# One decoder step on one core: common tile offsets, a turned output, uneven filling and another order of loads

## The reference, cut to what matters

```python
pp = in_proj(rmsnorm(x, norm_g), w_in, ...)            # 1024 -> 14 groups of columns
def block(i):                                          # forgetting attention: 8 heads x 64, blocks of 128 queries
    sc = einsum('bqhd,bkhd->bhqk', qb, k) * scale + cq[..., None] - c[:, :, None, :]
    sc = where(kpos[None, :] <= qpos[:, None], sc, -inf)
    p = softmax(sc, axis=-1)
    return einsum('bhqk,bkhd->bqhd', p, v)
o_hg, s = hgrn2(...)                                   # gated linear recurrence, 4 heads, state 128x128
o_mem = mem_attn(mem_q, mk, mv)                        # attention into 256 memory tokens
ya = (o_fox * silu(fox_z)) @ w_pa                      # and yb, ym likewise
mixed = sigmoid(ga) * ya + sigmoid(gb) * yb + sigmoid(gm) * ym
y = rmsnorm(x + mixed @ w_o, final_norm_g)
```

## Time and profile before

| | |
|---|---|
| median of three executions | 2919.84 us (2919.51 to 2931.8) |
| profiled execution | 2921.01 us, span 2919.3 |
| busy: TensorE | 2777.6 us, 95% |
| busy: VectorE, ScalarE, GpSimd | 1555.2, 1026.5, 766.0 us |
| mean granted TensorE clock | 0.986 |
| read from and written to HBM | 411 and 112 MB |

### The profile page before, as it was taken

How to read it: one execution, slowest core, us unless ns; L and a number is a source line. 1 busy time by engine, 2 the same in 40 slices (tenths; PEclk the granted TensorE clock), 3 DMA queues, 4 the chain that set the end, 5 groups by cost and what they waited for, 6 DMA issues and landing times.

```text
span 2919.3 us, 38536 instructions
## 1 busy us (share of the span) xinstructions
PE 2777.6 (95%) x13880; PEld 2279.4 (78%) x13880; DVE 1555.2 (53%) x2995; ACT 1026.5 (35%) x1946; POOL 766.0 (26%) x731
## 2 busy tenths in 40 slices
PE   7899998999999999899799999999999999999998
PEld 5778877777777878687688877888888877888887
DVE  6413566543442576765456555556554654544444
ACT  1211110333332444453355445455454332323231
POOL 6038775134225352523020041010020134000000
PEclk9999999999999999999999999999999999999999
DMA  5667678656646666655754565455344564333331
GB/s 174 227 234 228 224 241 282 247 170 187 190 156 218 207 203 222 213 186 192 239 177 131 158 200 166 145 173 164 120 155 173 195 228 165 112 123 109 126 104 41
DMA packets 285612, 525.78 MB, mean 180 GB/s; under 512 B 110238, under 2 KB 119007, under 8 KB 263151
## 3 DMA queue, kind: packets, MB, share of 16 engines
q1 hardware_dynamic: 226383, 309.16, 34.2%
q10 hardware_dynamic: 54720, 201.19, 19.8%
q0 software_dynamic: 4320, 12.98, 1.3%
HBM read 410.82 MB, written 112.41 MB: 179 GB/s over the span
## 4 chain that ended last, share of the span: by engine, by line
PE 70%; DMA 7%; POOL 6%; DVE 4%; issue 3%; SPq 3%; ACT 2%; ACTq 0%; POOLq 0%; DVEq 0%
PE fill_out L2623 21%; PE fox_o_sum L345 4%; PE fox_turned L391 4%; PE in_out L98 4%; PE in_out L100 4%; PE in_out L99 4%; PE mf_out L100 3%; PE mf_out L98 3%; PE mf_out L99 3%; POOL dc_slot L1660 2%; PE fox_scores L379 2%; DMA fill_x<-x_tiles 2%; PE mf_fin L98 2%; PE mf_fin L100 2%; PE mf_fin L99 2%
## 5 line engine op out<-in xcount | busy, mean ns | idle before, releaser
L2623 PE MATMUL fill_out<-keep_hi,fill_x 128*128 128x512 f32 x2112 | 734.8, 410 | 31.0 <-DMA fill_x<-x_tiles 15.8
L2623 PEld LDWEIGHTS fill_out<-keep_hi,fill_x 128*128 128x128 f32 x2112 | 386.2, 190 | 104.2 <-issue 20.8
L2623 PE MATMUL fill_out<-keep_lo,fill_x 128*128 128x512 f32 x1056 | 432.8, 410 | 0.0
L498 DVE TENSOR_TENSOR fox_pt_lo<-fox_turned,fox_pt_hi 128x512 fp32r<-128x512 f32 (+1 forms) x320 | 194.8, 609 | 183.5 <-ACT fox_pt_hi L443 181.6
L443 ACT ACTIVATE fox_pt_hi<-fox_turned 128x512 fp32r<-128x512 f32 (+1 forms) x320 | 169.9, 531 | 303.1 <-PE fox_turned L391 301.5
L2250 ACT ACTIVATE in_stage<-in_out 128x512 f32<-128x512 f32 (+1 forms) x119 | 70.9, 597 | 553.3 <-PE in_out L100 508.9
L2723 POOL CAST keep_hi<-fill_raw 128x512 fp32r<-128x512 f32 x72 | 48.8, 678 | 733.7 <-PE fill_out L2633 705.1
L484 DVE CUSTOM_DVE_ANT_0 fox_probs<-fox_scores,fox_bias 128x512 f32<-128x512 f32 (+2 forms) x320 | 187.5, 608 | 98.3 <-PE fox_scores L380 55.9
L2623 PEld LDWEIGHTS fill_out<-keep_lo,fill_x 128*128 128x128 f32 x1056 | 201.0, 190 | 31.8
L391 PE MATMUL fox_turned<-ident,fox_probs 128*128 128x128 f32 x1088 | 172.7, 274 | 14.9 <-ACT fox_probs L434 14.9
L391 PEld LDWEIGHTS fox_turned<-ident,fox_probs 128*128 128x128 f32 x1088 | 128.6, 140 | 44.9 <-ACT fox_probs L434 20.0
(11 more groups left out here) (395 smaller groups left out, 6396.8 us busy)
## 6 DMA issues: line engine op xcount, KB each, us to landing
fill_x<-x_tiles ACTq DMA_DIRECT2D x130, 1024.0 KB, 5.5
dc_slot<-in_cache_fox_k_dram SPq DMA_DIRECT2D x128, 256.0 KB, 3.7
dc_slot<-in_cache_fox_v_dram SPq DMA_DIRECT2D x128, 256.0 KB, 3.4
in_raw<-in_w_in_dram SPq DMA_DIRECT2D x104, 256.0 KB, 4.1
plain<-fill_stage ACTq DMA_DIRECT2D x96, 256.0 KB, 5.1
turned<-in_stage ACTq DMA_DIRECT2D x64, 256.0 KB, 3.8
fill_raw<-in_w_in_dram SPq DMA_DIRECT2D x56, 256.0 KB, 2.9
mf_g_in<-gated SPq DMA_DIRECT2D x51, 256.0 KB, 3.0
```

Source lines behind the costliest of these rows:

```text
L498: dve.tensor_tensor(pt_lo[:, b, skip:BANK], bank_of(st)[:, skip:BANK], pt_hi[:, b, skip:BANK].bitcast(F32), ALU.subtract).then_inc(turned_ ...
L2623: ins = pe.matmul(self.out[n % self.OUTS][:], x, w, start=(k == 0 and term == 0), stop=(ends and term == 2))
```

## The change

Four edits, independent of each other.

- **Offsets.** `bound` and `rest` become parts of one tile of 128 bytes; `xs_both` is followed by a tile of 448 bytes; `stat` moves behind the tiles that it shifted; in the attention `halves` goes and `pt_hi`, `pt_lo` and `o_turned` stand directly behind `probs`; `pages_begin` has 1024 bytes instead of 512. `keep_*`, `x_first`, `rest_*`, `fill_x`, all matmul operands of the attention and of the merge's products then start 256 bytes past a multiple of 512. `dc_pr` stays at 32 and 64 modulo 128.
- **Turning back.** L406's four matmuls become four transposes against the identity. VectorE copies the first halves of the four blocks to `o_rows`, adds the second halves, frees the bank, and then does its four products in place, from SBUF.
- **Filling.** `deal` gives the 1552 matmuls out by shares: 7 for the last slot of each quad, 2 for every other.
- **SyncE.** The loads of `w_o`'s slices move from GpSimd's queue to SyncE's: slices 0 and 1 once GpSimd has split the early weights, slices 2v+2 and 2v+3 at unit v, each waiting for the split of the slice two before. `load_g(3)` comes right behind `load_g(2)`. `load_w` 8 and 9 come at unit 1, 10 and 11 at unit 2.

```diff
-        self.bound, self.rest = (ctx.enter_context(nc.sbuf_tensor(n, [P, HH], F32)) for n in ("bound", "rest"))
+        limits = ctx.enter_context(nc.sbuf_tensor("limits", [P, LINE], F32))
+        self.bound, self.rest = limits[:, 0:HH], limits[:, HH:2 * HH]
...
-        fill.begin(first_matmuls + fill.spread(matmuls, 2 * FH * J_HEAD) + last_matmuls)
+        shares = [SEAM if st == ("key", st[1], st[2], 4 * st[2] + 3) and half else 2
+                  for st in steps if st[0] == "key" for half in range(2)]
+        fill.begin(first_matmuls + fill.deal(matmuls, shares) + last_matmuls)
...
+    def deal(matmuls, shares):
+        edges = [matmuls * sum(shares[:n]) // sum(shares) for n in range(len(shares) + 1)]
+        return [b - a for a, b in zip(edges, edges[1:])]
...
-                        last = pe.matmul(bank_of(st)[:, t * P:(t + 1) * P], o_turned[:, t * P:(t + 1) * P], halves[:],
-                                         start=True, stop=True)
+                        last = pe.transpose(bank_of(st)[:, t * P:(t + 1) * P], o_turned[:, t * P:(t + 1) * P],
+                                            core.ident[:])
...
+                    halves = bank_of(st)[:].rearrange("p (t u d) -> p t u d", u=2, d=FD)
+                    dve.tensor_copy(o_rows[n % 2][:], halves[:, :, 0, :]).then_inc(halves_added, 1)
+                    dve.wait_ge(halves_added, 2 * n + 1)
+                    dve.tensor_tensor(o_rows[n % 2][:], o_rows[n % 2][:], halves[:, :, 1, :], ALU.add
+                                      ).then_inc(halves_added, 1)
+                    dve.wait_ge(halves_added, 2 * n + 2)
+                    dve.sem_inc(turned_used, 1)
...
-                                                        in0=bank_of(st)[:, t * P:t * P + FD],
+                        last = dve.scalar_tensor_tensor(out=o_rows[n % 2][:, t, :], in0=o_rows[n % 2][:, t, :],
...
-                    dve.wait_ge(rows_ready, n + 1)
-                    dve.sem_inc(turned_used, 1)
...
+            def load_last(i):
+                kk, n = last_slices[i]
+                k = kk - NB * BT
+                if i >= 2:
+                    sp.wait_ge(late_split, 2 * i - 2)
+                sp.dma_start(late_raw[i % 2], w_o[k * P:(k + 1) * P, n * BANK:(n + 1) * BANK]
+                             ).then_inc(late_loaded[i % 2], 16)
...
+            sp.wait_ge(early_split, 2 * EARLY)
+            for i in range(2):
+                load_last(i)
...
             load_g(2)
+            load_g(3)
...
-                    if t == 0 and u == 0:
-                        for i in range(2 * BT, len(slices) - EARLY):
-                            load_w(i)
+                    if 1 <= v <= 2:
+                        for i in range(BT // 2):
+                            load_w((2 * BT + (v - 1) * BT // 2) + i)
...
-                    if u % HALVES == 1 and s + 3 < SEQ:
+                    if u % HALVES == 1 and 4 <= s + 3 < SEQ:
                         load_g(s + 3)
+                    for i in range(2 * v + 2, min(2 * v + 4, len(last_slices))):
+                        load_last(i)
...
-                if i + 2 < len(last_slices):
-                    pool.wait_ge(late_split, 2 * i + 2)
-                    load(i + 2)
...
+            held.enter_context(nc.sbuf_tensor("xs_end", [P, -KT * SAMPLE_COLUMNS % P], F32))
```

More of the change, by code:

```diff
@@ L31 @@
 BANK = 512
+LINE = 32
 NEG = -1e30
@@ L111, in attend_prompt @@
     S_BANKS, TURN_BANKS, PT_SLOTS = 2, 3, 4
-    SPREAD = 0.8
+    SPREAD, SEAM = 0.8, 7
     DEPTH = 2
@@ L175, in attend_prompt @@
         mask_r, ident_r = sb("mask_r", [P, P], F32R), sb("ident_r", [P, P], F32R)
-        halves = sb("halves", [P, P])
         probs = sb("probs", [P, PROBS])
+        pt_hi, pt_lo = sb("pt_hi", [P, PT_SLOTS, BANK], F32R), sb("pt_lo", [P, PT_SLOTS, BANK], F32R)
+        o_turned = sb("o_turned", [P, BANK])
         most = sb("most", [P, 8, CHUNKS[-1]])
@@ L181, in attend_prompt @@
         inverse = sb("inverse", [P, 4])
-        pt_hi, pt_lo = sb("pt_hi", [P, PT_SLOTS, BANK], F32R), sb("pt_lo", [P, PT_SLOTS, BANK], F32R)
-        o_turned = sb("o_turned", [P, BANK])
         def psum(name, n):
@@ L212, in attend_prompt @@
         o_copied, rows_ready = sem("o_copied"), sem("rows_ready")
-        started, inverse_ready = sem("started"), sem("inverse_ready")
+        started, inverse_ready, halves_added = sem("started"), sem("inverse_ready"), sem("halves_added")
         def slots_of(st):
@@ L316, in _ @@
             link(pool.memset(mask[:], 0.0))
-            link(pool.memset(halves[:], 0.0))
             pool.affine_select(out=mask[:], in_=mask[:], compare_op=ALU.is_ge, fill=NEG, base=0,
-                               pattern=[[-1, P]], channel_multiplier=1)
-            for n, base in enumerate((0, -FD, FD)):
-                link(pool.affine_select(out=halves[:], in_=halves[:], compare_op=ALU.not_equal, fill=1.0,
-                                        base=base, pattern=[[-1, P]], channel_multiplier=1))
+                               pattern=[[-1, P]], channel_multiplier=1).then_inc(masked, 1)
+            pool.wait_ge(masked, 1)
             link(pool.tensor_copy(mask_r[:], mask[:]))
@@ L509, in _ @@
                     dve.wait_ge(turned_ready, turn_at[st] + 1)
+                    halves = bank_of(st)[:].rearrange("p (t u d) -> p t u d", u=2, d=FD)
[5 more added lines that the diff above has]
+                    dve.sem_inc(turned_used, 1)
                     for t in range(4):
-                        last = dve.scalar_tensor_tensor(out=o_rows[n % 2][:, t, :],
-                                                        in0=bank_of(st)[:, t * P:t * P + FD],
+                        last = dve.scalar_tensor_tensor(out=o_rows[n % 2][:, t, :], in0=o_rows[n % 2][:, t, :],
                                                         scalar=inverse[:, t:t + 1], in1=z[n % 2][:, t, :],
@@ L2302, in normalise_and_project @@
         normed = [sb(f"normed{r}", [P, D]) for r in range(2)]
-        gains, memory_gains, stat = sb("gains", [P, D]), sb("memory_gains", [P, D]), sb("stat", [P, 2, 3])
+        gains, memory_gains = sb("gains", [P, D]), sb("memory_gains", [P, D])
         raw = [sb(f"raw{r}", [P, W]) for r in range(RAWS)]
@@ L2306, in normalise_and_project @@
         stage = [sb(f"stage{s}", [P, W]) for s in range(STAGES)]
+        stat = sb("stat", [P, 2, 3])
         turned = [ctx.enter_context(nc.psum_tensor(f"np_turned{r}", [P, KT, P], F32)) for r in range(TR)]
@@ L2575, in spread @@
         return [matmuls * (n + 1) // slots - matmuls * n // slots for n in range(slots)]
+    @staticmethod
+    def deal(matmuls, shares):
+        edges = [matmuls * sum(shares[:n]) // sum(shares) for n in range(len(shares) + 1)]
+        return [b - a for a, b in zip(edges, edges[1:])]
     def left(self):
@@ L2883, in merge_and_finish @@
         late_hi, late_lo = (sb(f"late_{n}", [P, len(slices) - EARLY, BANK], F32R) for n in ("hi", "lo"))
-        sb("pages_begin", [P, P])
+        sb("pages_begin", [P, 2 * P])
         early_hi, early_lo = (sb(f"early_{n}", [P, EARLY, BANK], F32R) for n in ("hi", "lo"))
@@ L2996, in _ @@
         def _(pool):
-            def load(i):
-                kk, n = last_slices[i]
-                k = kk - NB * BT
-                pool.dma_start(late_raw[i % 2], w_o[k * P:(k + 1) * P, n * BANK:(n + 1) * BANK]
-                               ).then_inc(late_loaded[i % 2], 16)
             def load_early(i):
@@ L3021, in _ @@
             pool.wait_ge(early_split, 2 * EARLY)
-            for i in range(2):
-                load(i)
             memory.multiplied(pool)
```

2 lines of the change are left out of this document (1 added, 1 removed).

## The result

The changed kernel takes 2907.69 us (median of 14 runs) against 2923.23 us of the kernel before on the same chip: a ratio of 0.9948, 95% interval 0.9936 to 0.996, or 15.2 us less (12 to 19). The forecast was 2882, with a range from 2864 to 2902. So it is faster, by under half of what was forecast, and the time lies outside the range. The kernel before took 2919.84 us when the prediction was made and 2923.23 in these runs, so some 3 us of the distance to 2882 are not the change's.

A forecast was written before the change was run, and what follows sets the result against it. The prediction took TensorE to bound the kernel; -17.8 - 14.0 + 2.5 - 9.0 + 0 = -38.3 took the profiled 2921.0 us to 2882.7, and with the median 1.2 lower to 2882 us, range 2864 to 2902.

The forecast's parts named there:

- What bounds the kernel: Whole kernel: TensorE holds 70% of the chain that ended last, no other engine more than 7%.
- Term 1: Common tile offsets for matmul operands throughout the kernel shorten the spacing between matmuls: -17.8 us.
- The 1702 inside: x 3.5 ns = 6.0 us: Attention: each of its 1702 fill matmuls gains 3.5 ns from common offsets, 6.0 us in all.
- the values product's 0.8: Attention: 640 matmuls of probabilities with values gain 1.2 ns each from common offsets, 0.8 us.
- its discount: Offsets' saving of 20.9 us of TensorE time: 15% left to stretches where it waits for something else.
- rival A: Offsets don't matter anywhere, so their gain is absent: 2899 us; chance 0.17.
- Term 2: Attention's back steps: transposes replace four products, -14.0 us on TensorE; the sum of halves moves to VectorE, +2.5 us.
- +2.5 on VectorE: Attention's back steps: VectorE's added copy and addition delay what is queued behind them, between 0 and 15 us, taken as +2.5.
- rival B: Attention: ScalarE and VectorE take the gain back, VectorE costing 12 us instead of 2.5: 2902 us; chance 0.13.
- In the short ones: Attention's short quads: scores come 2 to 3 a step, so some of VectorE's extra time shows.
- Term 3: Attention's quad seams: uneven filling covers TensorE's waits for the last exponential, -9.0 us, between -3 and -12.
- Term 4: Merge's begin: SyncE's new load order turns holes of 8.4 and 2.7 us into three smaller ones, 0 us.

The follow-up runs named there:

- the three kernels above: Tiles moved only, against the kernel before: starts 320 and 192 (2918.53 us against 2921.49), 0 and 256 (2906.42 against 2916.56), or the change's 256 and 256.
- kernel with late products: Kernel before plus offsets, transposes and filling, SyncE's order as before, VectorE's four products one key step later: 2886.97 us, ratio 0.9900.

## Why the prediction was wrong

The time lies 26 us above 2882. Some 3 of these are the slower kernel before; the gain itself was 15.2 us instead of 38.3. By the steps:

- **What bounds the kernel**: right, as far as shown. The offsets and the filling, which gave TensorE less to do or to wait for, gained; for the transposes alone the interval reaches just past 0.
- **Term 1, offsets, -17.8: the failed part is "The 1702 inside: x 3.5 ns = 6.0 us"** and the values product's 0.8. Outside the sum held by the rows: 4.4 ns for a kept fill matmul (233.4 to 229.0 in the recurrence) instead of 5.8, 6 in the projection and the first pass, about 12 us together, as forecast after its discount. In the attention, where 5.8 us were forecast after the discount, the profiles show 1.5 us for all its matmuls, within that stage's noise. That accounts for 4.3 of the 9.0 us by which the term missed: the timing has only 8.8, up to 12.6, of these 13.5 us, and what became of the rest stays open. The prediction took 227 ns as the spacing of tiles with one offset and 230 as that of the attention. Rows show something else, a merge run of tiles with one offset behind four transposes:

```profile
2501.51 0.60 PE L3057 MATMUL mf_turned<-ident,mf_g_in 128*128 128x128 f32 x4
2501.86 0.48 PE L100 MATMUL mf_out<-mf_early_hi,mf_t_hi 128*128 128x512 f32 x1
2502.17 0.40 PE L101 MATMUL mf_out<-mf_early_hi,mf_t_lo 128*128 128x512 f32 x1
...
2504.03 0.39 PE L100 MATMUL mf_out<-mf_early_hi,mf_t_hi 128*128 128x512 f32 x1
...
2504.49 0.39 PE L102 MATMUL mf_out<-mf_early_lo,mf_t_hi 128*128 128x512 f32 x1
...
2507.21 0.39 PE L102 MATMUL mf_out<-mf_late_lo,mf_t_hi 128*128 128x512 f32 x1
```

  The 8 steps from 2502.17 take 232.5 ns each, the 12 from 2504.49 226.7. Over all wide matmuls of this kernel's merge, by place behind the last transposes and without the long first step: the first four steps take 231.2 ns, the next four 229.7, the next four 227.8, later ones 226.7. In the attention 95% of such steps are among the first eight, and their mean is 231.0 ns before and 230.4 with the offsets: the first four go from 231.0 to 230.8, the next four from 230.9 to 229.2. The gain is for long runs. That a transpose before is the cause is read from the order of the rows, not tried. On record was also the sentence of the Trainium skill, "TensorE: Matmul & The Clock Gate", Part 2, on LDWEIGHTS: separate read ports for weights and streamed operand. What the prediction drew from it, that offsets are worth nothing, is decided by the measurement: the three kernels above show 227 or 233 by their place alone. So rival A is out. Whether it is the weights' reads that meet the streamed operand's, no run here shows.
- **Term 2, -14.0 on TensorE: right** (0.36 us a back; in the attention its matmuls fell from 25.8 to 11.6 us). **+2.5 on VectorE: the failed step is "I take +2.5 us, near the lower end because back follows the last scores of the shortest quad".** VectorE's idle time behind L406 fell from 42.7 to 28.7 us with the transposes, as said, but a back's copy, addition and products stand ahead of the maxima, and TensorE waits for these. Of the 14.2 us that the transposes save it, the attention shows 1.6 and so lost 12.6 (some 3 less if its length before is taken from the slower of the four executions with the same code); two thirds of that are longer steps to the scores' own matmuls. The timing says 10, 5 either way: 14.2 less the 4.1 measured. So it is four or five times the 2.5 taken, and near the 12 of rival B. "In the short ones" was the right place, but what shows there was most of it.
- **Term 3, -9.0: right**, -9.1. The waits for exponentials went from 14.9 us, 12 times, to 6.3, 6 times; those at the ends of heads 1, 5 and 6 stayed, start to start 1.6, 1.6 and 1.2 us, as worked out.
- **Term 4, 0: mis-sized by 4.7 us.** The waits are the forecast ones: start to start 5.4 for late_lo was 6.7, g(5) 3.4 was 1.5, g(6) 5.3 was 4.9, and fin waits for no slice. By its numbers the holes were to grow by 2.4 us (14.1 come, 11.7 go), and they grew by 2.3. What failed is "and the half clock after it (a matmul at 0.63 instead of 0.39) too", -2.0, with nothing put behind the new holes: matmuls at half clock cost 3.9 us in this stretch, 1.9 more than before. Holes and clock make 4.2 of the 4.4 us by which the merge is longer. The thirteen kernels with the old order in the merge take 518.3 to 523.1 us from its first to its last product, the three with the whole new order 525.2 to 526.1.

Of the signs that the prediction named, these came: fill matmuls at 227 ns in long runs, "back" at 0.36 us, VectorE's idle time before it 31.8 us, exponential waits of 7.1 us, no wait of 8 us in the merge. The group mean of the fill matmuls did not fall to 400 ns but stayed at 410, although their spacing fell from 233.4 to 229.0 in the recurrence: the mean duration of a row does not tell the spacing. The sign of being wrong, score waits above 15 us, depends on the row: 9.7 us for the matmuls, 25.2 for their weight loads.

Not in any term: the profiled execution of the changed kernel is the slowest of its 14, 5 us above their median, and waits 3.2 us in the attention for one late slice of the filler's weights:

```profile
1738.02 0.71 PE L2633 MATMUL fill_out<-keep_hi,fill_x 128*128 128x512 f32 x1 [3.21 <-POOL keep_lo L2742]
```

## What to carry to other kernels

Work moved to an engine that is half idle is not free: ask what stands behind it in that engine's order, and put what nobody waits for last. Here moving four products behind the next maxima took the whole change from -15.2 (-18.7 to -11.7) to -29.2 us (-38.6 to -20.2). Take a spacing from runs of the same length and neighbours as those it is applied to. And where one hole is traded for others, count the half clock behind the holes that come as well as behind those that go.

## What the runs showed of the hardware

- In long runs, fp32r matmuls of 128x512 whose two operands' starts in SBUF differ by 64 or 128 bytes, taken modulo 256 (192 and 256, 192 and 320), follow each other every 233 ns; those with no such difference (256 and 256, 320 and 320, 192 and 192, 0 and 256) every 227 to 228 ns. A difference of 256 costs nothing.
- Spacing is 230 to 231 ns for the first eight or so wide matmuls behind transposes and settles at 226.7 after some twelve, with operands at one place against 256. That the transposes are the cause was not tried.
- GpSimd took two products of 128x256 (797 and 613 ns) per back without slowing VectorE's 689 ns for pt_lo, which reads PSUM. VectorE's instructions with both inputs in SBUF do stretch while GpSimd splits weights. In the kernel with late products, where the products read SBUF, 13 of the 128 ran beside a split and took 616 ns on average, up to 1309, instead of 279. In the kernel before, where the same products read PSUM, 18 ran beside a split and took 278 ns, as the others. By the transposes the products had come to read SBUF; behind the maxima that harmed nothing.
